# Four tiles of the last stage's input loaded and split inside the attention stage, and ten of its first products issued there

## The chip, the cores and the metric

The kernel runs on one core of a Trainium2 chip. A core has a tensor engine (PE, with its weight loads as PEld), a vector engine (DVE), a scalar engine (ACT), GpSimd (POOL) and SyncE (SP), which here only issues DMAs. The metric is the device time of one execution in microseconds; lower is better.

## The reference

One decoder block with two branches over 2048 positions and 1024 channels, all in float32:

```python
def reference(x, norm_in, w_in, norm_v, w_s, b_s, w_o_gmlp, w_o_sb, w_out, norm_final):
    for layer in range(DEPTH):
        h = rms_norm(x, norm_in[layer])
        proj = jnp.einsum('bsd,de->bse', h, w_in[layer])
        u_a, v_a, z_a, q_b, k_b, v_b, z_b, gate_a, gate_b = jnp.split(proj, SPLIT_POINTS, axis=-1)
        ...
        y_a = chunked_spatial_gating(u_a, v_a, w_s[layer], b_s[layer]) * jax.nn.silu(z_a)
        ...
        y_b = stick_breaking_attention(heads(q_b), heads(k_b), heads(v_b)).reshape(bsz, seq, B_WIDTH)
        y_b = y_b * jax.nn.silu(z_b)
        p_a = jnp.einsum('bse,ed->bsd', y_a, w_o_gmlp[layer])
        p_b = jnp.einsum('bse,ed->bsd', y_b, w_o_sb[layer])
        merged = jax.nn.sigmoid(gate_a) * p_a + jax.nn.sigmoid(gate_b) * p_b
        x = x + jnp.einsum('bsd,de->bse', merged, w_out[layer])
    return rms_norm(x, norm_final)
```

The attention weight of query t for key s is sigmoid(z_ts) times the product of (1 - sigmoid(z_tj)) over the keys j between them.

## The kernel before

Three stages follow each other, each a block of its own; all engines meet at the end of a block. The first makes the norm, the input projection and branch A's mixing. The second, `attention`, makes the stick-breaking attention and, in between, branch A's output projection. The third, `merge_and_project_out`, makes p_b, merges, and projects out.

Every matrix product in float32 precision is three matmuls: each operand is split into a high half (rounded, made by ACT with a copy) and a low half (the rest, made by a subtraction on DVE or POOL), and high·high, high·low and low·high are added in PSUM. A "product" below is such a set of three, with 512 columns.

**Attention.** The work is 320 pieces (8 heads, four blocks of 512 queries taken from the last to the first, key blocks, four rows of 128 queries). All engines follow one list of events in slots. Slot n has event Z for piece n (the logits on PE, L1636 to L1638; two sigmoids on ACT; a scan on DVE, L1566 and L1576; the multiplication by the scanned product on POOL, L1488, after a mask on a diagonal piece), then B for piece n-6 (PE turns the weights, L1661; ACT copies the high half, L1542; DVE makes the low half, L1596), then P for n-8 (the product with v, L1672 to L1674). A turn of a group of four pieces waits until POOL has weighted all four. Behind the 320th piece there are eight more slots, in which only B and P are left. Event Y (L1604, DVE) gates the result of a query block, and SP stores it in `yb_T`.

Operands come through a ring of eight buffers (`RAWS`), as items: q, k, v, branch A's tokens and the weights `w_o_gmlp` ("w") and `w_o_sb` ("o"). SP loads an item when the one eight before it has been split. At the item's own slot (event K) ACT makes the high half (L1510) and POOL the low half (L1476); POOL follows the order of the events too. Items stand in the list `wanted` with the slot of each. The weights of p_b ("o") and two items of q are the last ones.

At the end of attention's program SP waits until all items are split, loads 128x2048 of `yb_T` (the first four tiles of y for the last stage, heads 0 to 3, the last 512 positions) into one wide buffer (L1459), and each of the last four events B is followed by one split of these: ACT's `split_first_chunk` (L1535) and DVE's `rest_of_first_chunk` (L1591).

**Last stage.** For each of four chunks c of 512 positions, from the last, PE adds eight tiles j of y into eight banks k: rows j = 0 to 5 over all k, then per bank j = 6, 7 (L2249 to L2251). DVE gates the banks (`gated_b`, L2153), POOL adds p_a (`add_a`, L1982), ACT issues the store of m_T (L2071). y tiles beyond the first four are loaded through a ring of four and split by ACT (`round_y`, L2044) and DVE (`rest_y`, L2137). POOL first makes four sets of sums of w_out (`w_sums`, L1971 to L1976); SP stores each set (`store_sums`, L1841) and POOL waits for that store before the next set. On SP stand in this order: y tiles 4 to 6 (L1822), w_out piece 0, the store of attention's last result, w_out piece 1, a wait for that store, y 7, eight gates, four p_a (L1832), sums 0, piece 2, sums 1, piece 3, y 8 to 11, sums 2, sums 3, y 12 to 14, the second four p_a, y 15. ACT makes y 4 to 10, then issues the eight stores of chunk 0, then makes y 11; DVE makes the low halves of y 4 to 10, then gates chunk 0. Numbers of y tiles count on over the chunks: y 8 to 15 are chunk 1's.

## Time and profile before

| | |
|---|---|
| median of 3 runs | 2566.29 us (2563.48 to 2568.18) |
| profiled execution | 2569.67 us, span 2568.0 us |
| mean granted clock of PE | 0.990 |
| busy: PE, PEld | 2492.1 us (97%), 2067.6 us (81%) |
| busy: DVE, ACT, POOL | 1596.0 us (62%), 1301.6 us (51%), 1258.3 us (49%) |
| attention ends, last stage starts | 2204.3 us from the span's start |

The span is from the first to the last instruction; the execution has 1.7 us around it. Matmuls are pipelined, so a matmul's own duration (0.39 us) is longer than the distance from one start to the next (0.23 us); distances between starts are what adds up.

### The profile page before, as it was taken

To read this page: it belongs to the slowest core of one execution; us is meant where nothing else is said; L and a number is where in the kernel's file an instruction comes from. 1 tells how busy PE (TensorE), PEld (TensorE's weight loads), DVE (VectorE), ACT (ScalarE), POOL (GpSimd) and SP (SyncE) were. 2 spreads that over 40 slices of the span, in tenths; PEclk is the share of its full clock that TensorE was granted. 3 is DMA by queue.
4 is the path that set the end of the run, shared out by engine and by line. 5 is a ranking of instruction groups with operands and counts; after the bars stand their busy time and mean duration, and the time that the engine had idled before them with its cause. 6 is when DMAs were issued, how large, how long until landed. Compare 5 with 4: busy or idle time off the path is not lost. (4 is left out here: it accounts for less than half of the span.)

```text
span 2568.0 us, 34996 instructions
## 1 busy us (share of the span) xinstructions
PE 2492.1 (97%) x11925; PEld 2067.6 (81%) x11925; DVE 1596.0 (62%) x2091; ACT 1301.6 (51%) x2372; POOL 1258.3 (49%) x1127
## 2 busy tenths in 40 slices
PE   7999999999989999999999999999999999989898
PEld 5788888888878888888888778888888887768687
DVE  7545555554575555555555588878788888332676
ACT  6664333334355444443444387767777778211343
POOL 2543332322335544444343378667866777432564
PEclk9999999999999999999999999999999999999899
DMA  3333333333334345554444434334433433668543
GB/s 123 98 98 119 119 102 115 110 106 122 103 90 127 115 132 151 147 146 144 132 140 127 160 107 141 89 92 138 136 97 106 129 113 101 213 232 276 205 149 113
DMA packets 280633, 338.02 MB, mean 132 GB/s; under 512 B 16408, under 2 KB 181280, under 8 KB 280480
## 3 DMA queue, kind: packets, MB, share of 16 engines
q1 hardware_dynamic: 276880, 329.58, 41.5%
q10 hardware_dynamic: 3600, 6.56, 0.7%
q8 instruction: 77, 1.26, 0.2%
q14 instruction: 76, 0.62, 0.1%
HBM read 222.83 MB, written 113.25 MB: 131 GB/s over the span
## 5 line engine op out<-in xcount | busy, mean ns | idle before, releaser
L1028 PE MATMUL in_bank<-carried_hi,in_w_hi 128*128 128x512 f32 x1988 | 783.4, 394 | 13.1 <-DVE carried_last L822 8.3
L1031 PE MATMUL in_bank<-carried_hi,in_w_lo 128*128 128x512 f32 x1988 | 775.4, 390 | 0.0
L1030 PE MATMUL in_bank<-carried_lo,in_w_hi 128*128 128x512 f32 x1988 | 775.2, 390 | 0.0
L1028 PEld LDWEIGHTS in_bank<-carried_hi,in_w_hi 128*128 128x128 f32 x1988 | 374.1, 188 | 91.9 <-DVE carried_last L822 9.7
L1031 PEld LDWEIGHTS in_bank<-carried_hi,in_w_lo 128*128 128x128 f32 x1988 | 373.9, 188 | 78.9
L1030 PEld LDWEIGHTS in_bank<-carried_lo,in_w_hi 128*128 128x128 f32 x1988 | 374.3, 188 | 74.9
L548 ACT ACTIVATE in_w_hi<-in_sums 128x512 fp32r<-128x512 f32 x284 | 178.6, 630 | 470.1 <-PE in_bank L1031 316.4
L1576 DVE TENSOR_TENSOR_SCAN att_rest<-att_z_ps,att_rest 128x512 f32<-128x512 f32 (+3 forms) x288 | 317.2, 1102 | 47.5 <-ACT att_z_ps L1522 28.6
L417 POOL TENSOR_TENSOR in_sums<-carried_stage 128x512 f32<-128x512 f32 x71 | 97.1, 1367 | 438.7 <-DMA carried_stage<-in_w_in 419.4
L753 DVE TENSOR_TENSOR in_w_lo<-in_sums,in_w_hi 128x512 fp32r<-128x512 f32 x284 | 269.0, 948 | 54.7 <-ACT in_w_hi L548 48.6
L822 DVE TENSOR_TENSOR carried_last<-in_bank,in_o 128x512 f32<-128x512 f32 x71 | 49.1, 691 | 304.6 <-PE in_bank L1031 55.0
L753 DVE TENSOR_TENSOR in_w_lo<-carried_stage,in_w_hi 128x512 fp32r<-128x512 f32 x213 | 214.4, 1007 | 23.5 <-ACT in_w_hi L548 21.5
L548 ACT ACTIVATE in_w_hi<-carried_stage 128x512 fp32r<-128x512 f32 x213 | 133.7, 628 | 144.8 <-PE in_bank L1031 73.3
L1488 POOL TENSOR_TENSOR carried_wide<-carried_wide,att_rest 128x512 f32<-128x512 f32 (+3 forms) x160 | 151.2, 947 | 92.2 <-DVE att_rest L1576 87.5
L1476 POOL TENSOR_TENSOR carried_lo<-carried_wide,carried_hi 128x512 fp32r<-128x512 f32 x152 | 195.4, 1293 | 0.0
L1596 DVE TENSOR_TENSOR att_wT_lo<-att_t_ps,att_wT_hi 128x512 fp32r<-128x512 f32 (+1 forms) x320 | 187.9, 588 | 4.7 <-ACT att_wT_hi L1542 4.4
L1542 ACT ACTIVATE att_wT_hi<-att_t_ps 128x512 fp32r<-128x512 f32 (+1 forms) x320 | 170.4, 533 | 5.1 <-PE att_t_ps L1661 4.8
L1522 ACT ACTIVATE att_z_ps<-att_z_ps 128x512 f32<-128x512 f32 (+2 forms) x320 | 171.3, 535 | 0.0
L1521 ACT ACTIVATE carried_wide<-att_z_ps 128x512 f32<-128x512 f32 (+3 forms) x160 | 85.3, 533 | 83.1 <-PE att_z_ps L1638 82.7
L1672 PE MATMUL att_y_ps<-att_wT_hi,carried_hi 128*128 128x512 f32 (+1 forms) x320 | 120.9, 378 | 3.8 <-DVE carried_wide L1604 2.0
L1636 PE MATMUL att_z_ps<-carried_hi 128*128 128x512 f32 (+2 forms) x320 | 118.1, 369 | 5.0 <-PEq L46 3.7
L1684 PE MATMUL att_f_ps<-carried_hi 128*128 128x512 f32 x256 | 122.1, 477 | 0.0
(215 smaller groups left out, 4787.4 us busy)
## 6 DMA issues: line engine op xcount, KB each, us to landing
carried_stage<-in_w_in SPq DMA_DIRECT2D x144, 512.0 KB, 4.8
carried_wide<-ya_T SPq DMA_DIRECT2D x64, 256.0 KB, 3.4
uz_T<-in_o SPq DMA_DIRECT2D x32, 256.0 KB, 4.6
carried_wide<-va_T SPq DMA_DIRECT2D x16, 512.0 KB, 5.7
carried_wide<-uz_T SPq DMA_DIRECT2D x16, 512.0 KB, 6.3
ya_T<-in_x_sb SPq DMA_DIRECT2D x16, 512.0 KB, 5.0
carried_wide<-k_T SPq DMA_DIRECT2D x32, 256.0 KB, 3.3
carried_wide<-q_T SPq DMA_DIRECT2D x32, 256.0 KB, 3.5
```

The costliest lines, as they stand in the source:

```text
L548: act.activation(w_hi[:, i], left[i], ACT.Copy).then_inc(w_hi_done[i], 1)
L753: dve.tensor_tensor(w_lo[:, i], left[i], w_hi[:, i].bitcast(F32), ALU.subtract)\
L1028: pe.matmul(bank[:, :], hi, a_hi[:, i, k], start=opens and k == 0, stop=False, skip_group_check=True)
L1030: pe.matmul(bank[:, :], hi, a_lo[:, i, k], start=False, stop=False, skip_group_check=True)
L1031: mm = pe.matmul(bank[:, :], lo, a_hi[:, i, k], start=False, stop=k == HALF_K - 1, skip_group_check=True)
L1476: pool.tensor_tensor(lo, src, hi.bitcast(F32), ALU.subtract).then_inc(split_done, 1)
L1488: pool.tensor_tensor(a, a, rest[r][:, left + 1:left + width + 1], ALU.mult).then_inc(weighted, 1)
L1522: act.activation(src, src, ACT.Sigmoid, scale=-SCALE).then_inc(rest_done, 1)
L1542: act.activation(wT_hi[m % W_BUFS][:, c0:], bank_of(step)[:, c0:], ACT.Copy).then_inc(hi_copied, 1)
L1576: dve.tensor_tensor_scan(out=row[:, left:left + width][:, ::-1], data0=z_ps[n % Z_BANKS][:, 0:width][:, ::-1], data1=row[:, S:S + 1].to_br ...
L1596: dve.tensor_tensor(wT_lo[b][:, c0:], bank_of(step)[:, c0:], wT_hi[b][:, c0:].bitcast(F32), ALU.subtract).then_inc(lo_copied, 1)
L1684: pe.matmul(f_ps[:, :], wo_hi[:, j, cols], ya_hi[:, j], start=j == 0, stop=False)
```

## The change

The first four tiles of y become items of attention's ring ("y", at slots 306, 309, 317 and 312 for tiles 0, 1, 2, 3), each loaded alone; ACT makes the high half at that slot and POOL the low half. The wide load and the splits behind the last four events B go away. Ten of the first 64 products of the last stage (tile j, bank k) become events M on PE in slots 311, 313, 316 and 320 to 326, each at the end of its slot, into banks 0 to 3. For this the eight PSUM banks are shared by all stages; the last stage's bank 0 is attention's `f_ps`, banks 1 to 3 its `z_ps`. The last stage leaves these ten out, and its counters of split y tiles start at tile 4.

```diff
+FIRST_Y = [306, 309, 317, 312]
+EARLY_M = {(0, 0): 311, (1, 0): 313, (3, 0): 316, (2, 0): 320, (0, 1): 321, (0, 2): 322, (0, 3): 323, (1, 1): 324,
+           (1, 2): 325, (1, 3): 326}
...
+        for j in range(QT):
+            wanted.append((FIRST_Y[j], ("y", j, 0)))
...
+            order += [("M", jk) for jk, at_slot in EARLY_M.items() if at_slot == slot]
...
+    if which == "y":
+        return s["yb_T"][m * P:(m + 1) * P, S - CW:S]
...
+    if which == "y":
+        return carried.first_chunk(m)
...
-        z_ps = [sc.ps(f"z_ps{n}", [P, CW]) for n in range(Z_BANKS)]
-        t_ps = [sc.ps(f"t_ps{n}", [P, CW]) for n in range(T_BANKS)]
-        y_ps, f_ps = sc.ps("y_ps", [P, CW]), sc.ps("f_ps", [P, CW])
+        z_ps, t_ps = carried.banks[:Z_BANKS], carried.banks[Z_BANKS:Z_BANKS + T_BANKS]
+        y_ps, f_ps = carried.banks[-2:]
...
+                if item[0] == "y":
+                    for n in range(ZBS):
+                        sp.wait_ge(y_stored[n], 16 * len(range(n, item[1] * NSUP + 1, ZBS)))
...
-            last_sup = range((HEADS - 1) * NSUP + 1)
-            for n in range(ZBS):
-                sp.wait_ge(y_stored[n], 16 * len(last_sup[n::ZBS]))
-            sp.wait_ge(split_done, len(splits))
-            sp.wait_ge(split_first, len(by_vector))
-            sp.wait_ge(turned, max(w.step_of["V", item] for item in w.items if item[0] == "v") + 1)
-            first_y = carried.buffer[1].rearrange("p (j t) -> p j t", j=QT)
-            sp.dma_start(first_y, s["yb_T"].rearrange("(j p) t -> p j t", p=P)[:, 0:QT, S - CW:S])\
-                .then_inc(carried.y_loaded, 16)
...
+                elif which == "y":
+                    place = FIRST_PLACES[m]
+                    act.wait_ge(z_full, w.last_logits(("qk"[place // QT], HEADS - 1, place % QT)) + 1)
...
-                if m >= len(w.turns) - QT:
-                    split_first_chunk(m - len(w.turns) + QT)
...
-                if m >= len(w.turns) - QT:
-                    rest_of_first_chunk(m - len(w.turns) + QT)
...
+            def first_chunk(j, k):
+
+                if k == 0:
+                    pe.wait_ge(f_done, BLOCKS)
+                else:
+                    pe.wait_ge(scanned, max(n for n in range(len(w.pieces)) if n % Z_BANKS == k - 1) + 1)
+                wait_split(pe, ("y", j, 0), ("o", k, j // (KT // 2)))
+                bank, cols = [f_ps, *z_ps][k], slice(k * P, (k + 1) * P)
+                y_hi, y_lo = carried.first_chunk(j)
+                opens = (j, k) == next(jk for jk in EARLY_M if jk[1] == k)
+                pe.matmul(bank[:, :], wo_hi[:, j, cols], y_hi, start=opens, stop=False, skip_group_check=True)
+                pe.matmul(bank[:, :], wo_hi[:, j, cols], y_lo, start=False, stop=False, skip_group_check=True)
+                pe.matmul(bank[:, :], wo_lo[:, j, cols], y_hi, start=False, stop=False, skip_group_check=True)
...
-        banks = [sc.ps(f"bank{i}", [P, CW]) for i in range(BANKS)]
+
+        banks = [carried.banks[-1], *carried.banks[:-1]]
...
-                sp.wait_ge(y_lo_done, n - RING + 1)
+                if n >= RING + QT:
+                    sp.wait_ge(y_lo_done, n - RING + 1 - QT)
...
+                        if c == 0 and (j, k) in EARLY_M:
+                            continue
```

GpSimd's own order, at slots 304 to 308. Before, L1488 is the weighting of a piece, L1484 the mask, L1476 the low half of an item (here of "o"):

```order
L1488 TENSOR_TENSOR carried_stage<-carried_stage,att_rest 128x512 x2
L1476 TENSOR_TENSOR carried_lo<-carried_wide,carried_hi 128x4x128
L1488 TENSOR_TENSOR carried_wide<-carried_wide,att_rest 128x512
L1488 TENSOR_TENSOR att_slot<-att_slot,att_rest 128x512
L1476 TENSOR_TENSOR carried_lo<-carried_wide,carried_hi 128x4x128
```

With the change the same operations are L1494 and L1482:

```order
L1494 TENSOR_TENSOR carried_stage<-carried_stage,att_rest 128x512 x2
L1482 TENSOR_TENSOR carried_lo<-carried_wide,carried_hi 128x4x128
L1494 TENSOR_TENSOR carried_wide<-carried_wide,att_rest 128x512
L1482 TENSOR_TENSOR carried_lo<-carried_wide,carried_hi 128x512
L1494 TENSOR_TENSOR att_slot<-att_slot,att_rest 128x512
L1482 TENSOR_TENSOR carried_lo<-carried_wide,carried_hi 128x4x128
```

The low half of y's tile 0 (the 128x512 row) now stands between the weighting of pieces 306 and 307; those of tiles 1 and 3 stand likewise behind pieces 309 and 312, that of tile 2 behind piece 317.

The tensor engine's order, from the turn of piece 316 (slot 322) on. Before, L1661 turns (one row of this list per source tile), L1672 to L1674 are one product with v:

```order
L1661 MATMUL att_t_ps<-carried_ident,carried_wide 128x128
L1661 MATMUL att_t_ps<-carried_ident,att_slot 128x128 x2
L1661 MATMUL att_t_ps<-carried_ident,carried_last 128x128
L1672 MATMUL att_y_ps<-att_wT_hi,carried_hi 128x512
L1673 MATMUL att_y_ps<-att_wT_lo,carried_hi 128x512
L1674 MATMUL att_y_ps<-att_wT_hi,carried_lo 128x512
L1661 MATMUL att_t_ps<-carried_ident,att_slot 128x128 x2
L1661 MATMUL att_t_ps<-carried_ident,carried_last 128x128
```

With the change the turns are L1655, the products with v L1666 to L1668, and the new events M L1692 to L1694:

```order
L1655 MATMUL carried_bank<-carried_ident,carried_wide 128x128
L1655 MATMUL carried_bank<-carried_ident,att_slot 128x128 x2
L1655 MATMUL carried_bank<-carried_ident,carried_last 128x128
L1666 MATMUL carried_bank<-att_wT_hi,carried_hi 128x512
L1667 MATMUL carried_bank<-att_wT_lo,carried_hi 128x512
L1668 MATMUL carried_bank<-att_wT_hi,carried_lo 128x512
L1692 MATMUL carried_bank<-carried_hi 128x512
L1693 MATMUL carried_bank<-carried_lo,carried_hi 128x512
L1694 MATMUL carried_bank<-carried_hi,carried_lo 128x512
L1655 MATMUL carried_bank<-carried_ident,att_slot 128x128 x2
L1655 MATMUL carried_bank<-carried_ident,carried_last 128x128
```

A product of the last stage now stands between the product of piece 314 and the turn of piece 317. The same holds after the products of pieces 315, 316, 317 and 318; one more M stands right ahead of the turn of piece 316 (slot 321), and one right ahead of the turn of piece 315 (slot 320).

## Rows read from the trace of the kernel before

**Rows 1.** The page's first part: busy us, share, instructions.

```profile
PE 2492.1 (97%) x11925; PEld 2067.6 (81%) x11925; DVE 1596.0 (62%) x2091; ACT 1301.6 (51%) x2372; POOL 1258.3 (49%) x1127
```

**Rows 2.** Busy time by stretch: stretch, its length, each engine's busy us (instructions).

```profile
core 0: us, PE busy (x) PEld busy (x) DVE busy (x) ACT busy (x) POOL busy (x), PEclk, DMA share, GB/s
2158.30:2192.90 34.60, 31.20 (x172) 24.84 (x171) 31.10 (x44) 30.23 (x67) 34.09 (x37) 1.00 0.21 61
...
2204.30:2248.30 44.00, 43.81 (x193) 36.01 (x193) 6.50 (x9) 4.43 (x7) 15.83 (x13) 1.00 0.79 277
2248.30:2265.00 16.70, 16.60 (x72) 13.40 (x72) 4.03 (x7) 0.00 (x0) 10.07 (x8) 1.00 0.61 205
2265.00:2274.20 9.20, 0.01 (x1) 0.01 (x1) 0.76 (x2) 1.42 (x3) 4.92 (x4) 0.65 0.66 245
2274.20:2280.00 5.80, 5.80 (x18) 4.66 (x19) 2.43 (x4) 1.41 (x3) 0.00 (x0) 0.68 0.62 180
```

**Rows 3.** The tensor engine's waits in the last stage: total us, times, longest.

```profile
PE b_bank L2260 <- DVE carried_wide L2182: 11.2, 1, 11.2
PE b_bank L2249 <- DVE carried_lo L2137: 9.3, 1, 9.3
```

**Rows 4.** The chain that ended last, 2204 to 2275 us: start, us, what.

```profile
2204.32 0.32 SPq L1822
...
2206.11 7.31 DMA yb_T<-carried_wide
...
2221.33 8.71 DMA w_sums<-b_sums
...
2246.42 4.27 DMA w_sums<-b_sums
...
2255.94 5.04 POOL carried_wide L1982 x4
...
2263.00 6.43 DMA carried_wide<-pa_T
...
2273.44 1.90 DVE carried_lo L2137 x3
```

**Rows 5.** DVE in order of time: start, us, count, idle before it.

```profile
2203.34 0.69 DVE L1604 TENSOR_TENSOR carried_wide<-att_y_ps,carried_wide 128x512 f32<-128x512 f32 x1
...
2247.47 4.86 DVE L2153 TENSOR_TENSOR carried_wide<-b_bank,carried_wide 128x512 f32<-128x512 f32 x8
```

**Rows 6.** GpSimd's groups of instructions, 2158.3 to 2197.2 us.

```profile
L1476 POOL TENSOR_TENSOR carried_lo<-carried_wide,carried_hi 128x512 fp32r<-128x512 f32 x12 | 15.5, 1296 | 0.0
```

**Rows 7.** GpSimd in order of time, its last pieces of attention.

```profile
2187.91 1.28 POOL L1476 TENSOR_TENSOR carried_lo<-carried_wide,carried_hi 128x512 fp32r<-128x512 f32 x1
2189.14 2.15 POOL L1488 TENSOR_TENSOR carried_stage<-carried_stage,att_rest 128x512 f32<-128x512 f32 x2
...
2194.00 0.87 POOL L1488 TENSOR_TENSOR att_slot<-att_slot,att_rest 128x384 f32<-128x384 f32 x1 [0.77 <-DVE att_rest L1576]
...
2196.06 1.09 POOL L1488 TENSOR_TENSOR carried_last<-carried_last,att_rest 128x512 f32<-128x512 f32 x1 [0.94 <-DVE att_rest L1576]
```

**Rows 8.** The tensor engine in order of time, attention's last turns and products.

```profile
2197.35 0.27 PE L1661 MATMUL att_t_ps<-carried_ident,carried_wide 128*128 128x128 f32 x1
...
2199.62 0.27 PE L1661 MATMUL att_t_ps<-carried_ident,carried_last 128*128 128x128 f32 x1
2200.65 0.47 PE L1672 MATMUL att_y_ps<-att_wT_hi,carried_hi 128*128 128x512 f32 x1 [0.76 <-DVE carried_wide L1604]
...
2202.30 0.28 PE L1674 MATMUL att_y_ps<-att_wT_hi,carried_lo 128*128 128x256 f32 x1
2202.75 0.33 PE L1672 MATMUL att_y_ps<-att_wT_hi,carried_hi 128*128 128x128 f32 x1 [0.17 <-DVE att_wT_lo L1596]
...
2204.35 0.47 PE L2249 MATMUL b_bank<-carried_hi 128*128 128x512 f32 x1 [1.05 <-PEq L1354]
```

**Rows 9.** DVE's group of the first four tiles' low halves, 2197 to 2204.3 us.

```profile
L1591 DVE TENSOR_TENSOR carried_lo<-carried_wide,carried_hi 128x512 fp32r<-128x512 f32 x4 | 2.7, 679 | 0.0
```

More of the change, by code:

```diff
@@ L162, in norm_and_project @@
         v_mean, v_rms = (sc.sb(n, [P, NT]) for n in ("v_mean", "v_rms"))
-        banks = [sc.ps(f"bank{i}", [P, CW]) for i in range(BANKS)]
+        banks = carried.banks
         stage = carried.as_weights(0)
@@ L1258, in in_slots @@
                 wanted.append((free, ("o", c, part)))
-        wanted.sort(key=lambda w: (w[0], w[1][1], -w[1][2], "kqvawo".index(w[1][0])))
+        for j in range(QT):
+            wanted.append((FIRST_Y[j], ("y", j, 0)))
+        wanted.sort(key=lambda w: (w[0], w[1][1], -w[1][2], "kqvawoy".index(w[1][0])))
         self.items = [item for _, item in wanted]
@@ L1529, in copy_v @@
                 act.activation(halves_of(carried, item)[0], bank_of(step)[:, :], ACT.Copy).then_inc(hi_copied, 1)
-            def split_first_chunk(i):
-                src, hi, _ = carried.first_chunk(i)
-                act.wait_ge(carried.y_loaded, 16)
-                act.wait_ge(z_full, len(w.pieces))
-                act.activation(hi, src, ACT.Copy).then_inc(carried.y_hi_done, 1)
             def copy_weights(m):
@@ L1586, in rest_of_v @@
                 dve.tensor_tensor(lo, bank_of(step)[:, :], hi.bitcast(F32), ALU.subtract).then_inc(lo_copied, 1)
-            def rest_of_first_chunk(i):
-                src, hi, lo = carried.first_chunk(i)
-                dve.wait_ge(carried.y_hi_done, i + 1)
-                dve.tensor_tensor(lo, src, hi.bitcast(F32), ALU.subtract).then_inc(carried.y_lo_done, 1)
             def rest_of_weights(m):
@@ L1690, in _ @@
                     logits(i)
+                elif e == "M":
+                    first_chunk(*i)
                 elif e == "V":
@@ L1751, in merge_and_project_out @@
         minus_half = sc.sb("minus_half", [P, 1])
-        banks = [sc.ps(f"bank{i}", [P, CW]) for i in range(BANKS)]
+        banks = [carried.banks[-1], *carried.banks[:-1]]
         bank_a, bank_b, bank_c = ([banks[3 * b + j] for b in range(2)] for j in range(3))
@@ L1785, in merge_and_project_out @@
         y_loaded, gate_loaded, pa_loaded = sc.sems("y_loaded", RING), sc.sems("gate_loaded", KT), sc.sems("pa_loaded", RING)
-        y_hi_done, y_lo_done = carried.y_hi_done, carried.y_lo_done
+        y_hi_done, y_lo_done = sc.sem("y_hi_done"), sc.sem("y_lo_done")
         row_done, full, gated, added = (sc.sem(n) for n in ("row_done", "full", "gated", "added"))
@@ L1859, in load_m @@
                 if n == 0:
-                    sp.wait_ge(y_lo_done, TILES_Y)
+                    sp.wait_ge(y_lo_done, TILES_Y - QT)
                 elif n == 1:
@@ L2135, in rest_y @@
             def rest_y(n):
-                dve.wait_ge(y_hi_done, n + 1)
+                dve.wait_ge(y_hi_done, n + 1 - QT)
                 dve.tensor_tensor(y_half(1, n), y_raw[n % RING], y_half(0, n).bitcast(F32), ALU.subtract)\
@@ L2248, in outer @@
                 n = KT * c + j
-                pe.matmul(banks[k][:, :], wo(0, j, k), y_half(0, n), start=j == 0, stop=False, skip_group_check=True)
+                opens = j == 0 and (c > 0 or k not in (of for _, of in EARLY_M))
+                pe.matmul(banks[k][:, :], wo(0, j, k), y_half(0, n), start=opens, stop=False, skip_group_check=True)
                 pe.matmul(banks[k][:, :], wo(0, j, k), y_half(1, n), start=False, stop=False, skip_group_check=True)
@@ L2267, in _ @@
                 for j in range(BY_HEAD):
-                    pe.wait_ge(y_lo_done, KT * c + j + 1)
+                    wait_past(pe, y_lo_done, max(0, KT * c + j + 1 - QT))
                     for k in range(KT):
@@ L2276, in _ @@
                         if k == 0:
-                            pe.wait_ge(y_lo_done, KT * c + j + 1)
+                            pe.wait_ge(y_lo_done, KT * c + j + 1 - QT)
                         mm = outer(c, j, k)
@@ L2325, in __init__ @@
         self.ident = sc.sb("ident", [P, P])
+        self.banks = [sc.ps(f"bank{i}", [P, CW]) for i in range(BANKS)]
         self.not_older = sc.sb("not_older", [P, P])
@@ L2335, in __init__ @@
         self.y_stored = sc.sems("y_stored", ZBS)
-        self.y_loaded, self.y_done, self.y_hi_done, self.y_lo_done = (
-            sc.sem(n) for n in ("y_loaded", "y_done", "y_hi_done", "y_lo_done"))
+        self.y_done = sc.sem("y_done")
     def first_chunk(self, i):
@@ L2342, in first_chunk @@
         cols = slice(place % 4 * CW, (place % 4 + 1) * CW)
-        return [self.buffer[1][:, i * CW:(i + 1) * CW], self.hi[:, place // 4, cols], self.lo[:, place // 4, cols]]
+        return [half[:, place // 4, cols] for half in (self.hi, self.lo)]
     def as_tiles(self, n):
```

## Prediction, made before the changed kernel ran

> **What bounds the kernel now.** I first read the page: the tensor engine is busy for 97% of the span [rows 1]. That is an average, and the change works at one seam, so I then read busy time by stretch around the end of attention, the waits of the tensor engine behind it, the chain of work that ended last, and each engine in order of time.
>
> In the last 35 us of attention's pieces the engine without a pause is not the tensor engine but GpSimd: 34.09 us busy of 34.60, against 31.20 for PE [rows 2]. All of this stretch's weighting and splitting queues there, and PE's turns wait for it.
>
> In the last stage PE runs without a gap for 44 us, for another 16.7 us with a hardly visible one, and then stands still for 9.2 us [rows 2, 3]. What it waits for is tile 11 of y, the fourth of chunk 1. The chain shows why that tile is late, and none of it is PE: SP's first issue at 2204.32, the store of attention's last result (7.31 us), SP's further issues, the store of the first sums (8.71 us), GpSimd's sums and their stores in turns until 2255.94, four additions of p_a, the load of the next four p_a (6.43 us), their additions, ACT's stores, and the split of tile 11 at 2273.44 [rows 4]. The chain begins with the block itself; nothing in it waits for a product of chunk 0. From there on PE is the bound except for one wait of 11.2 us, for the first output sums [rows 3], which hangs on the chunks before it.
>
> So there are two clocks. The end of attention moves everything behind it. What PE saves between 2204 and 2265 is not worth anything, as it only comes earlier to the wait for tile 11.
>
> **What is saved in the last stage.** In that stage PE makes 193 matmuls in 44.00 us, one per 0.228 us [rows 2]. Ten products are thirty matmuls, 6.84 us. Chunk 0 would be done 6.8 us earlier after the stage's start, at about 2241.4 on the old scale. But chunk 1's first product needs bank 0 gated, and DVE starts that at 2247.47, right behind the low half of tile 10 [rows 5], whose load SP issues in its fixed order. PE so waits there for some 7 us, makes three rows, and then waits for tile 11 as before. If the clock falls in the first wait, as it does in the 9.2 us one (granted clock 0.65, and 0.68 in the 5.8 us behind it, which is the 1.2 GHz level for a part of them [rows 2]), the rows behind it take some 2 us longer, and there are 9 us of waiting to hide that. Term: 0. If that cover were not there, the term would be -6.8.
>
> The order of loads changes nothing here: y 4 to 7 had their buffers free before too, and the counters for y 8 on ask for the same tiles.
>
> **GpSimd's four low halves.** One costs 1.296 us by its own record [rows 6]; from one start to the next instruction's it is 1.23 (2187.91 to 2189.14 [rows 7]). I take 1.24. In the stretch in which tiles 0, 1 and 3 are inserted (behind pieces 306, 309, 312) GpSimd is never idle for long, so the weighting of piece 315 is 3 x 1.24 = 3.7 us later. Tile 2's half stands behind piece 317. There GpSimd waits twice for scans, 0.77 and 0.94 us [rows 7], and those scans hang on piece 319's logits, which PE makes behind the turn of piece 312, thus behind the weighting of piece 315: from the end of that one (2189.14 + 2.15 = 2191.29) to the end of the last (2196.06 + 1.09 = 2197.15) it is 5.86 us, of which GpSimd works 5.86 - 1.71 = 4.15. With 1.24 more it works 5.4, which fits. So the fourth costs nothing, and the last weighting moves by 3.7. Bounds: 5.0 if all four count, 0 if the queue had slack. Queued behind GpSimd are PE's turns, and behind these ACT and DVE.
>
> What this takes off DVE is four low halves of 0.679 us [rows 9], and four copies off ACT. They lie in the last 6 us, where DVE and ACT wait for PE's turns in between; the gating that product 316 waits for comes at most 0.2 us earlier by it. Bounds 0 to 1; I take 0.
>
> The Trainium skill's GPSIMD Engine Reference (Engine selection) advises VectorE for elementwise work on a tile, since GpSimd takes about twice as long for two inputs. The trace agrees: 1296 ns against 679 ns for the same subtraction. By that rule alone the four halves would cost 4 x 0.6 = 2.5 us more of engine time, whoever waits for it.
>
> **PE behind the last weighting.** Before, from the turn of piece 316 (2197.35) to the last product (2202.75) there are 5.40 us. Two waits are in it, by starts: 2199.62 + 0.11 to 2200.65 is 0.92, 2202.30 + 0.12 to 2202.75 is 0.33 [rows 8]. PE works 4.15 us. The change puts five products (slots 322 to 326) between these, 5 x 0.684 = 3.4 us, and one (slot 321) right ahead of the turn of piece 316, where PE arrives just as the weighting ends: 0.7 us. The first wait shrinks to some 0.2 us, because it is what is left of the time from product 315 to the gating of its block's result (0.92 and 0.23 of piece 318's turn, 1.15), and now a product and the turn lie in that (0.68 + 0.23); the second goes. New length 0.7 + 4.15 + 3.4 + 0.2 = 8.45, against 5.40: 3.05 us later. The products of slots 311, 313, 316 and 320 are hidden: PE has 3.4 us of gaps in the 34.6 before [rows 2] and now waits more for GpSimd. Bounds: 4.1 if no wait shrinks, about 2.3 if the turn of 316 doesn't find PE occupied.
>
> **The sum.** Attention ends 3.7 + 3.05 = 6.75 us later. The last gated result starts at 2203.34 [rows 5] and the stage's first matmul at 2204.35 [rows 8], 1.0 us apart with the meeting of the engines between them; this distance stays. The last stage keeps its length. The profiled execution of 2569.67 would become 2576.4; it stands 3.4 us above the median 2566.29, to which the same difference is added: 2573.0 us, slower by 0.26%.
>
> **The rivals.**
> - *GpSimd has slack after all* (its pieces are due later than I think, so that its late halves don't reach PE): only the 3.05 us of the tail stay, 2569.3. For it: PE is 31.2 us busy of 34.6, so it doesn't wait much. Against it: a queue with 0.5 us of idle time in 34.6 has nothing to take 5 us in. It decides if the weighting of piece 319 ends less than 1.5 us later. Chance 0.12.
> - *The saving shows in the last stage too, and pays the seam*: 6.75 - 6.84, 2566.2. That would need the wait for tile 11 to follow PE, not SP. For it: 97% of PE in the span. Against it: the chain [rows 4]. Chance 0.08.
> - *Faster*: the seam's work lies in PE's waits (they sum to 3.4 us in the stretch and 1.3 in the tail) and the thirty matmuls leave the path behind it. If chunk 0's end is what releases chunk 1's gating, and so tile 11, each product saved counts 0.68 us; it turns faster by over 0.2% when attention's end moves by less than 1.7 us. With an end that doesn't move: 2559.5. Against it: DVE's gating began at 2247.47 right behind a low half, before PE had asked for it. Chance 0.06. The Trainium skill's Perfetto Trace Analysis (Optimization Strategy) says that interleaving regimes with different bounds may gain; this rival is that rule at work, and the trace speaks against it, as the regime that receives the work has a full queue on GpSimd.
> - *The clock*: the new wait of 7 us and the old one stand 16 us apart. If PE stays at the lower clock in the rows between, or longer behind tile 11, each 4 us at it cost 2 us. Behind tile 11 that is not hidden: 2575 to 2577. Chance 0.08.
> - *My forecast*, 0.66, with a range of its own of 2570.0 to 2576.0.
>
> **How the numbers follow.** What a measurement of this kernel can tell from no change is about 0.2%, 5.1 us; the three runs spread over 4.7 us. Slower by that is above 2571.4. Of the forecast's 0.66 about 0.50 lies above it, since the tail or the queue may be 1.5 us shorter than I make it; with the clock's 0.08 that is 0.58. Within 0.2%: 0.16 of the forecast, 0.12 and 0.08, 0.36. Faster 0.06. The range reaches down to the rival without a change, less some noise, 2565.5, and up to the clock's 2577.0; about 0.1 stays out on either side.
>
> **What would show it.** Right, if in the changed kernel GpSimd is busy without a gap from 2158 to about 2196 and its last weighting ends near 2201; if DVE's last gating of attention starts near 2210 and the last stage's first matmul near 2211; if PE has a new wait of 6 to 8 us there, released by DVE's gating of chunk 0, and still 7 to 10 us for tile 11, which ends near 2281; and if the stretch from the stage's first matmul to the end is as long as before within 1.5 us. Wrong, if the last stage is shorter by several us: then something in SP's chain followed PE. Wrong in the first term, if GpSimd shows waits among pieces 306 to 317, and in the second, if PE's gaps behind the last weighting stay.

## The result and the profile after

The changed kernel takes 2573.11 us (median of 8 runs, 2571.66 to 2575.56) against 2566.11 us of the kernel before (8 runs, the three on record among them, 2563.11 to 2570.37): 7.0 us slower, a ratio of 1.0028 with a 95% interval of 1.0018 to 1.0037. The profiled execution took 2574.6 us with a span of 2572.9 us.

This profile ran 2.6 us ahead of the one before when it reached the change. 2.5 of it was there when attention's first matmul started (1474.69 against 1477.18 us), and in the fourteen profiles that start lies anywhere from 1474.69 to 1479.78, with the change and without. So I compare distances, not places. GpSimd in order of time, before and then after, with piece 305 (the second of the x2 in the first row) as the common mark, since the first new item comes behind it:

```profile
2171.01 2.17 POOL L1488 TENSOR_TENSOR carried_stage<-carried_stage,att_rest 128x512 f32<-128x512 f32 x2
```

```profile
2168.44 2.15 POOL L1494 TENSOR_TENSOR carried_stage<-carried_stage,att_rest 128x512 f32<-128x512 f32 x2
...
2172.85 1.28 POOL L1482 TENSOR_TENSOR carried_lo<-carried_wide,carried_hi 128x512 fp32r<-128x512 f32 x1
...
2190.29 2.15 POOL L1494 TENSOR_TENSOR carried_stage<-carried_stage,att_rest 128x512 f32<-128x512 f32 x2
...
2194.11 1.28 POOL L1482 TENSOR_TENSOR carried_lo<-carried_wide,carried_hi 128x512 fp32r<-128x512 f32 x1
...
2197.22 1.09 POOL L1494 TENSOR_TENSOR carried_last<-carried_last,att_rest 128x512 f32<-128x512 f32 x1 [0.39 <-DVE att_rest L1577]
```

Before, piece 305's weighting ends at 2173.18 and the last weighting at 2197.15 [rows 7], 23.96 us apart (from unrounded times). After, it is 2170.59 to 2198.31, 27.72: GpSimd's part of attention's end is 3.76 us longer. The low half of tile 0 (2172.85) and its neighbours stand in a queue with no pause; that of tile 2 (2194.11) stands where the waits of 0.77 and 0.94 us were [rows 7], and only one of 0.39 is left.

The tensor engine in order of time behind the last weighting (L1655 turns, L1666 to L1668 products with v, L1692 to L1694 the new ones, L2263 the last stage):

```profile
2199.20 0.27 PE L1655 MATMUL carried_bank<-carried_ident,carried_wide 128*128 128x128 f32 x1
...
2202.85 0.27 PE L1655 MATMUL carried_bank<-carried_ident,carried_last 128*128 128x128 f32 x1
2203.09 0.47 PE L1666 MATMUL carried_bank<-att_wT_hi,carried_hi 128*128 128x512 f32 x1
...
2206.70 0.39 PE L1694 MATMUL carried_bank<-carried_hi,carried_lo 128*128 128x512 f32 x1
2206.93 0.22 PE L1666 MATMUL carried_bank<-att_wT_hi,carried_hi 128*128 128x128 f32 x1
...
2208.43 0.47 PE L2263 MATMUL carried_bank<-carried_hi 128*128 128x512 f32 x1 [1.05 <-PEq L1367]
```

From the turn of piece 316 to the last product it is 2199.20 to 2206.93, 7.73 us, against 5.40 [rows 8]; the turn comes 0.89 us behind the last weighting, against 0.20. The wait of 0.92 us by starts is now 2202.85 + 0.11 to 2203.09, 0.13, and the other is gone. DVE in order of time shows attention's last gating (L1598) and the first of chunk 0 (L2166):

```profile
2207.41 0.69 DVE L1598 TENSOR_TENSOR carried_wide<-carried_bank,carried_wide 128x512 f32<-128x512 f32 x1 [1.95 <-PE carried_bank L1668]
...
2251.89 4.87 DVE L2166 TENSOR_TENSOR carried_wide<-carried_bank,carried_wide 128x512 f32<-128x512 f32 x8
```

From the last weighting to the last gating it is 9.10 us against 6.19: the tail is 2.91 us longer. Together attention ends 6.67 us later, and the first matmul stands 1.02 us behind that gating as before.

Busy time by stretch in the last stage, and the tensor engine's waits there:

```profile
core 0: us, PE busy (x) PEld busy (x) DVE busy (x) ACT busy (x) POOL busy (x), PEclk, DMA share, GB/s
...
2208.30:2252.30 44.00, 37.00 (x162) 30.33 (x162) 5.77 (x8) 4.42 (x7) 15.19 (x13) 0.95 0.80 280
2252.30:2271.50 19.20, 18.78 (x71) 15.32 (x72) 4.46 (x8) 0.00 (x0) 10.53 (x9) 0.84 0.66 227
```

```profile
PE carried_bank L2274 <- DVE carried_wide L2195: 11.0, 1, 11.0
PE carried_bank L2263 <- DVE carried_wide L2166: 9.6, 2, 7.3
PE carried_bank L2263 <- DVE carried_lo L2150: 5.8, 1, 5.8
```

The first 44 us hold 162 matmuls instead of 193 [rows 2], and the last stage has a new wait of 7.3 us for the gating of chunk 0. The other part of the 9.6 us is the wait for the gating of chunk 1: 2.3 us, ending 101.3 us behind the stage's first matmul, against 2.15 us and 101.2 before. The wait for tile 11 is 5.8 us instead of 9.3 [rows 3] and ends 69.4 us behind the stage's first matmul, against 69.8. The stage takes 364.5 us from its first matmul to the end, against 363.6. So the saving of 6.84 us is there in PE's work and nowhere in the time. Against the profile before, the sum is 6.67 + 0.86 - 2.6 = 4.9 us, the difference of the spans.

### The profile page after: what moved, and what is told of

It reads as the page before. It is cut to its first block and busy times, and to the rows that moved or that the text cites. A ratio compares the mean times of both kernels' runs of the same rounds, so it can differ in the third digit from the quotient of the medians.

```text
span 2572.9 us, 35013 instructions
## 1 busy us (share of the span) xinstructions
PE 2497.2 (97%) x11925; PEld 2071.5 (81%) x11925; DVE 1593.6 (62%) x2087; ACT 1302.9 (51%) x2372; POOL 1270.1 (49%) x1131
## 5 line engine op out<-in xcount | busy, mean ns | idle before, releaser
L1028 PE MATMUL carried_bank<-carried_hi,in_w_hi 128*128 128x512 f32 x1988 | 783.8, 394 | 11.1 <-DVE carried_last L822 8.2
L1031 PE MATMUL carried_bank<-carried_hi,in_w_lo 128*128 128x512 f32 x1988 | 775.9, 390 | 0.0
L1030 PE MATMUL carried_bank<-carried_lo,in_w_hi 128*128 128x512 f32 x1988 | 775.5, 390 | 0.0
L1028 PEld LDWEIGHTS carried_bank<-carried_hi,in_w_hi 128*128 128x128 f32 x1988 | 374.4, 188 | 89.5 <-DVE carried_last L822 9.7
L1031 PEld LDWEIGHTS carried_bank<-carried_hi,in_w_lo 128*128 128x128 f32 x1988 | 374.2, 188 | 78.9
L1030 PEld LDWEIGHTS carried_bank<-carried_lo,in_w_hi 128*128 128x128 f32 x1988 | 374.6, 188 | 75.2
L1577 DVE TENSOR_TENSOR_SCAN att_rest<-carried_bank,att_rest 128x512 f32<-128x512 f32 (+3 forms) x288 | 317.5, 1103 | 48.2 <-ACT carried_bank L1531 28.9
L1482 POOL TENSOR_TENSOR carried_lo<-carried_wide,carried_hi 128x512 fp32r<-128x512 f32 x156 | 200.4, 1292 | 0.0
L1494 POOL TENSOR_TENSOR carried_wide<-carried_wide,att_rest 128x512 f32<-128x512 f32 (+3 forms) x160 | 151.1, 946 | 91.7 <-DVE att_rest L1577 87.1
L1592 DVE TENSOR_TENSOR att_wT_lo<-carried_bank,att_wT_hi 128x512 fp32r<-128x512 f32 (+1 forms) x320 | 188.6, 590 | 7.2 <-ACT att_wT_hi L1545 6.8
L1545 ACT ACTIVATE att_wT_hi<-carried_bank 128x512 fp32r<-128x512 f32 (+1 forms) x320 | 170.5, 533 | 9.1 <-PE carried_bank L1655 8.9
L1531 ACT ACTIVATE carried_bank<-carried_bank 128x512 f32<-128x512 f32 (+2 forms) x320 | 171.2, 535 | 0.0
L1666 PE MATMUL carried_bank<-att_wT_hi,carried_hi 128*128 128x512 f32 (+1 forms) x320 | 120.8, 377 | 2.3 <-DVE carried_wide L1598 1.3
```

The source lines that it names most:

```text
L1028: pe.matmul(bank[:, :], hi, a_hi[:, i, k], start=opens and k == 0, stop=False, skip_group_check=True)
L1030: pe.matmul(bank[:, :], hi, a_lo[:, i, k], start=False, stop=False, skip_group_check=True)
L1031: mm = pe.matmul(bank[:, :], lo, a_hi[:, i, k], start=False, stop=k == HALF_K - 1, skip_group_check=True)
L1482: pool.tensor_tensor(lo, src, hi.bitcast(F32), ALU.subtract).then_inc(split_done, 1)
L1494: pool.tensor_tensor(a, a, rest[r][:, left + 1:left + width + 1], ALU.mult).then_inc(weighted, 1)
L1531: act.activation(src, src, ACT.Sigmoid, scale=-SCALE).then_inc(rest_done, 1)
```

## The experiments

Each kernel ran in turns with the kernel before. One profile's last stage varies by some us between executions even where its code is the same: e2 and the change have the same last stage, with 359.9 and 364.5 us. Up to e9 the part behind the wait for the first output sums is always 154.7 to 155.8 us long; what varies is when that wait ends, 204.5 to 209.3 us behind the stage's first matmul. So a difference of less than some 5 us in one profile's last stage says nothing by itself. The ratio judges the whole, and the profile's distances judge attention's end, which repeats within 0.05 us. A "lock" below is a wait that ends when it did, whatever work of PE ahead of it is taken away. In the table these are: from the end of piece 305's weighting to the end of the last weighting; from there to the last gating's start; from the stage's first matmul to the end of the span. The ratio is to the kernel before.

| kernel | us, median | ratio, 95% interval | queue | tail | last stage |
|---|---|---|---|---|---|
| before | | | 23.96 | 6.19 | 363.6 |
| change | 2573.11 | 1.0028 (1.0018 to 1.0037) | 27.72 | 9.10 | 364.5 |
| e1_no_early | 2569.25 | 1.0007 (0.9997 to 1.0016) | 27.75 | 5.72 | 361.7 |
| e2_low_dve | 2573.25 | 1.0029 (1.0017 to 1.0040) | 25.69 | 9.12 | 359.9 |
| e3_four_early | 2570.12 | 1.0017 (1.0007 to 1.0026) | 27.73 | 5.74 | 359.5 |
| e4_left_out | 2565.65 | 0.9993 (0.9983 to 1.0002) | 23.99 | 6.19 | 361.1 |
| e5_act_order | 2568.85 | 1.0004 (0.9994 to 1.0013) | 23.98 | 6.19 | 360.2 |
| e6_act_order_after | 2573.49 | 1.0021 (1.0011 to 1.0030) | 27.73 | 9.13 | 360.6 |
| e8_loads_before | 2567.33 | 1.0000 (0.9990 to 1.0009) | 23.96 | 6.20 | 363.3 |
| e9_loads_after | 2572.56 | 1.0016 (1.0006 to 1.0025) | 27.74 | 9.10 | 363.4 |
| e10_w_later_before | 2559.49 | 0.9973 (0.9963 to 0.9984) | 23.96 | 6.19 | 356.2 |
| e11_w_later_after | 2568.41 | 1.0003 (0.9994 to 1.0013) | 27.73 | 9.10 | 357.4 |
| e12_w_later_four | 2567.18 | 1.0004 (0.9994 to 1.0013) | 30.93 | 5.73 | 357.1 |
| e13_w_later_four_pool | 2565.52 | 0.9991 (0.9982 to 1.0001) | 27.74 | 5.75 | 356.5 |

The kernel before that ran beside them had medians of 2566.11 us (change), 2566.75 (e1 to e4), 2567.36 (e5 to e9), 2566.03 (e10 to e12) and 2567.16 (e13).

**The two terms apart.** No early products at all:

```diff
-EARLY_M = {(0, 0): 311, (1, 0): 313, (3, 0): 316, (2, 0): 320, (0, 1): 321, (0, 2): 322, (0, 3): 323, (1, 1): 324,
-           (1, 2): 325, (1, 3): 326}
+EARLY_M = {}
```

> The change without its ten early products (the table of them is empty; the last stage makes all 64 again); the four y tiles stay items of attention's ring with low halves by GpSimd. Two-term theory (GpSimd's queue 3.7 us, products in the tail 3.0 us): only GpSimd's term is left, attention's last weighting still ends 3.7 us later against piece 305, the last gated result 3.2 to 3.7 us later (DVE and ACT lack the old splits in the tail), the last stage is as long as before; time 3.5 us above before, 3.5 below the change. Rival A (the products alone cost, GpSimd has slack): as before, 2566. Rival B (the products pay in the last stage and GpSimd costs all of it): not below the change, 2573 or more.

The queue stays 3.79 us longer, the tail is 0.47 us shorter than before. GpSimd's first and last rows of the distance, and DVE's last gating (L1597):

```profile
2168.93 2.15 POOL L1493 TENSOR_TENSOR carried_stage<-carried_stage,att_rest 128x512 f32<-128x512 f32 x2
...
2197.73 1.09 POOL L1493 TENSOR_TENSOR carried_last<-carried_last,att_rest 128x512 f32<-128x512 f32 x1 [0.37 <-DVE att_rest L1576]
```

```profile
2204.54 0.69 DVE L1597 TENSOR_TENSOR carried_wide<-carried_bank,carried_wide 128x512 f32<-128x512 f32 x1 [0.64 <-PE carried_bank L1667]
```

Attention ends 3.3 us later. The time, 2.5 us above before by the medians with an interval of the ratio of -0.8 to 4.1, agrees with that and is clear of the change. Both rivals fall: the queue shows that GpSimd has no slack (the time alone would still allow no difference), and the time lies below the change, so the products do cost. The 0.47 us is what went with the four old splits on ACT and DVE; I had taken 0.

With only the four early products that I had called hidden:

```diff
+EARLY_M = {(0, 0): 311, (1, 0): 313, (3, 0): 316, (2, 0): 320}
```

> The change with only four early products, those of slots 311, 313, 316 and 320; the six of slots 321 to 326 go back to the last stage. Two-term theory: these four lie in waits, so it is as the change without any: last weighting 3.7 us later, tail no longer than before (5.2 to 5.4 us from the turn of piece 316 to the last product, change 8.3), time 3.5 us above before and equal to the kernel without early products within 0.5 us. Rival (each of the ten costs alike, 0.3 us apiece, as PE is 97% busy): 1.2 us above the kernel without.

The queue is 27.73 and the tail 5.74, within 0.02 us of the kernel without any; the time is 0.9 us above that one's, less than the two intervals can tell apart. These four cost nothing in attention, and the six of slots 321 to 326 cost all of the 3.4 us by which the tails of change and e3 differ.

Low halves of y by DVE at the same slots (a counter of its own, `y_low`, on which PE and SP wait for these items):

```diff
+                if e == "K" and i[0] == "y":
+                    hi, lo = halves_of(carried, i)
+                    dve.wait_ge(split_hi, hi_of[i] + 1)
+                    dve.tensor_tensor(lo, raw_of(i)[0], hi.bitcast(F32), ALU.subtract).then_inc(y_low, 1)
```

> The change with the four low halves of y made by DVE at the same slots instead of GpSimd; the ten early products stay. Two-term theory: GpSimd's queue is relieved of 4 x 1.24 us, DVE gets 4 x 0.59 us with 3.5 us of idle time in that stretch; the last weighting is 0 to 1 us later than before (change: 3.7), the tail is 3.0 us longer as in the change; the last gated result 3.0 to 4.0 us later than before, time 3.5 us above before. Rival A (GpSimd has slack): no better than the change, 2573. Rival C (DVE is as full, the scans come late): 6 us above before.

This missed. The queue shrinks from 27.72 to 25.69, but is still 1.73 us longer than before, more than the 0 to 1 expected; the tail is 9.12. The time is 6.5 us above before (interval 4.4 to 10.3) instead of 3.5, and no better than the change. The rows of GpSimd and DVE show where the 1.73 us come from:

```profile
2171.46 2.59 POOL L1500 TENSOR_TENSOR carried_stage<-carried_stage,att_rest 128x512 f32<-128x512 f32 x2
...
2177.36 1.75 POOL L1488 TENSOR_TENSOR carried_lo<-carried_wide,carried_hi 128x512 fp32r<-128x512 f32 x1
...
2184.85 1.41 POOL L1500 TENSOR_TENSOR carried_wide<-carried_wide,att_rest 128x512 f32<-128x512 f32 x1
...
2190.80 2.15 POOL L1500 TENSOR_TENSOR carried_stage<-carried_stage,att_rest 128x512 f32<-128x512 f32 x2
```

```profile
2172.03 1.07 DVE L1618 TENSOR_TENSOR carried_lo<-carried_wide,carried_hi 128x512 fp32r<-128x512 f32 x1
...
2177.27 0.69 DVE L1618 TENSOR_TENSOR carried_lo<-carried_wide,carried_hi 128x512 fp32r<-128x512 f32 x1
...
2184.56 0.74 DVE L1618 TENSOR_TENSOR carried_lo<-carried_wide,carried_hi 128x512 fp32r<-128x512 f32 x1
```

Each of these three subtractions overlaps an instruction of GpSimd, and that instruction is longer than its like in the change: 2.59, 1.75 and 1.41 us instead of 2.15, 1.28 and 1.09, 1.2 us together. By as much the weighting of pieces 314 and 315 starts late: 19.34 us behind that of 304 and 305, against 18.13 before. Behind it GpSimd loses 0.9 us more, with a new wait of 0.72 us for a scan of DVE. So all of it is 2.1 us; piece 305's end, the mark of the table, hides 0.4 us, since its own row is one of the longer ones.

**Is PE's saving worth anything in the last stage?** The kernel before with the ten products left out altogether, so that its p_b lacks them (the first product left in each bank opens it):

```diff
+LEFT_OUT = [(0, 0), (1, 0), (2, 0), (3, 0), (0, 1), (0, 2), (0, 3), (1, 1), (1, 2), (1, 3)]
...
+                        if c == 0 and (j, k) in LEFT_OUT:
+                            continue
```

> The kernel before, whose last stage leaves out the ten products (tiles 0 to 3 into banks 0 to 3) altogether, so that p_b lacks them for the first chunk; attention is untouched. Theory (the wait for tile 11 hangs on SP, GpSimd and the stores): no gain, time within 1.5 us of before; a new wait of 6 to 8 us on DVE's gating of chunk 0, and the wait for tile 11 ends at the same distance from the stage's start, 69 to 70 us. Rival (the last stage follows PE): 6.8 us below before, 2559.

It is 1.1 us below before, with an interval of -4.4 to 0.5 us; a gain of 6.8 us is excluded. The tensor engine's waits in the last stage:

```profile
PE b_bank L2262 <- DVE carried_wide L2183: 10.1, 1, 10.1
PE b_bank L2250 <- DVE carried_wide L2154: 8.0, 2, 6.6
PE b_bank L2250 <- DVE carried_lo L2138: 6.9, 1, 6.9
```

The work left out has become a wait of 6.6 us for the gating of chunk 0. The wait for tile 11 ends 68.6 us behind the stage's first matmul (69.8 before), and that for the gating of chunk 1 at 100.1 (101.2 before). So even work that vanishes, with no cost elsewhere, had gained only 1.1 us by then.

**Which lock is it?** On ACT in the last stage, tile 11 goes ahead of the stores:

```diff
             for n in range(4, 11):
                 round_y(n)
-            for k in range(KT):
+            round_y(11)
+            for k in range(RING):
                 store_m(0, k)
-            for n in range(11, 16):
+            for n in range(12, 15):
                 round_y(n)
+            for k in range(RING, KT):
+                store_m(0, k)
+            round_y(15)
```

> The kernel before with one reordering on ACT in the last stage: the split of tile 11 stands ahead of the eight stores of chunk 0, tiles 12 to 14 between the fourth and the fifth, tile 15 behind them. Theory (tile 11 is late because ACT's stores wait for the additions of p_a): the wait for tile 11 of 9.3 us goes, and the last stage gets 6 to 10 us shorter, unless the wait before the first output sums (11.2 us, about 205 us behind the stage's start) grows by what is gained; time 2557 to 2560. Rival (tile 11 is late for its load or for DMA bandwidth): no change, 2566. Rival 2 (the later wait grows by the same): 2566 with that wait at 18 to 20 us.

This missed: there is no gain (1.5 us above, interval -1.5 to 3.3), though the mechanism worked: tile 11 is ready 48.5 us behind the stage's start instead of 69.8, and PE never waits for it. Its waits now:

```profile
PE b_bank L2253 <- DVE carried_wide L2157: 11.5, 1, 11.5
PE b_bank L2264 <- DVE carried_wide L2186: 8.4, 1, 8.4
```

The 9.3 us moved into the wait for the gating of chunk 1 (2.15 us before), which now ends 98.8 us behind the start. It was neither of the two waits that I had thought of. The same reordering on the changed kernel:

> The changed kernel with the same reordering on ACT. Theory: its last stage has the same gain, but the wait for the gating of chunk 0 (7.3 us) stays, for that hangs on the loads of tiles 8 to 10; so it stands 6.7 us above the kernel before with the reordering, as without it. Rival (with tile 11 out of the way the ten early products pay): equal to the kernel before with the reordering within 1.5 us.

It stands 4.6 us above e5 by the medians (4.4 by the ratios), attention ends 6.7 us later, and it has both the 7.2 us wait for chunk 0's gating and one of 9.5 us for chunk 1's.

Then SP's loads, on both kernels: tiles 8 to 10 right behind tile 7, tile 11 behind w_out's piece 2, tiles 12 to 14 behind piece 3.

```diff
             load_y(7)
+            for n in range(8, 11):
+                load_y(n)
...
             load_piece(2)
+            load_y(11)
             store_sums(1)
             load_piece(3)
-            for n in range(8, 12):
-                load_y(n)
+            for n in range(12, 15):
+                load_y(n)
             store_sums(2)
             store_sums(3)
-            for n in range(12, 15):
-                load_y(n)
```

> The kernel before with the reordering on ACT and SP's loads of tiles 8 to 10 right behind that of tile 7, tile 11 behind w_out's piece 2, tiles 12 to 14 behind piece 3. Theory: DVE can gate chunk 0 as soon as PE closes its banks; for the kernel before this is worth nothing over the reordering alone (PE met no wait there), 0 to 1 us either way. Rival (the earlier loads delay the sums of w_out on the full DMA queues): some us slower than the reordering alone.

> The changed kernel with both, the reordering on ACT and the earlier loads of y. Theory: only here nothing is left to wait for in the first two chunks, so the thirty matmuls moved out of the last stage count, 6.8 us, against 6.7 us of later attention end: equal to the kernel before with both within 1.5 us, its waits after the stage's start at about 44 and 69 us gone. Rival (another chain holds the last stage, the sums of w_out or the stores of m_T): 6.7 us above the kernel before with both, with the wait before the first output sums grown by 6 to 7 us.

e8 equals before. In e9 the wait at 44 us is gone, as expected, and the kernel is still 5.2 us above e8 by the medians, 4.1 by the ratios. With the width of the two intervals that leaves room for a part of the saving, so the waits have to decide:

```profile
PE carried_bank L2268 <- DVE carried_wide L2171: 16.6, 1, 16.6
PE carried_bank L2279 <- DVE carried_wide L2200: 11.0, 1, 11.0
PE carried_bank L2268 <- DVE carried_lo L2155: 1.7, 1, 1.7
```

e8 waits 11.3 us for the gating of chunk 1. There are 16.6 - 11.3 + 1.7 = 7.0 us of new waits: the 6.84 us saved, all of it. The rival was right that another chain holds the stage, though not in which: the wait before the first output sums did not grow (11.0 us, e8 11.7). The lock that takes everything ahead of it is the gating of chunk 1. In before, the change and e1 to e9 PE's wait for it ends 98.6 to 101.8 us behind the stage's first matmul, whatever was changed ahead of it; the waits at 44 and 70 us were only its forerunners.

**Moving that lock.** On ACT the splits of w_out's blocks for chunks 1 and 2 go behind the six y tiles, on DVE behind the gating too:

```diff
-                for i in (P1, P6) if c == 1 else (P2,):
-                    rest_w(i)
                 for j in range(BY_HEAD):
                     rest_y(KT * (c + 1) + j)
                 for k in range(KT):
                     gated_b(c, k)
+                for i in (P1, P6) if c == 1 else (P2,):
+                    rest_w(i)
```

> The kernel before with tile 11 ahead of the stores on ACT, the earlier loads of y on SP, and on ACT and DVE the splits of w_out's blocks for chunks 1 and 2 behind the six y tiles (on DVE behind the gating too). Theory (the gating of chunk 1, about 100 us behind the stage's start, is the lock on which all savings ahead of it are lost; it is late because on ACT and DVE the two blocks of w_out stand ahead of y 16 to 21 and the gating): the wait of 11.3 us at 99 us shrinks to 2 to 4 us, the last stage is 7 to 9 us shorter, 2558 to 2560. Rival (a later lock, the wait before the first output sums at 205 us, takes it back): 2566, with that wait near 18 us.

It takes 2559.49 us, 0.9973 (0.9963 to 0.9984): the fastest of all, 6.5 us below before. Its waits:

```profile
PE b_bank L2265 <- DVE carried_wide L2187: 9.8, 1, 9.8
PE b_bank L2254 <- DVE carried_wide L2158: 6.3, 1, 6.3
```

11.3 us became 6.3, less than I expected to be taken off, and the wait before the first output sums did not grow. In this profile ACT's split ahead of the gating waits 19 us for loads of y that SP issues behind the two blocks of w_out. So the lock has moved by 5 us (the wait ends 93.6 us behind the start instead of 98.6) and is still one. The other 2 us of the 7.1 by which the stage is shorter than e8's go with the wait before the first output sums (9.8 us instead of 11.7), and are within what that varies by. The changed kernel with the same:

> The changed kernel with the same three. Theory: with the locks loosened a part of the 6.8 us saved on PE can count; but what is left as a wait in the kernel before with the three (2 to 4 us) shows that the loads are nearly as late, so only that remainder is missed: 3 to 6.7 us above the kernel before with the three. Rival (nothing else holds): equal to it within 1.5 us. Rival 2 (a lock remains and takes all): 6.7 us above it.

It is 8.9 us above e10, 7.7 us by the ratios. Attention's end is 6.7 us of it; the last stage shows no saving (357.4 us, against 356.2), with a wait of 10.1 us for the gating of chunk 1, which ends at 92.4 us. I had expected 3 to 6.7; the second rival holds, the lock still takes all.

The changed kernel with the same three, the four hidden products alone and y's low halves by DVE:

> The changed kernel with the same three, only the four early products that lie in waits, and y's low halves by DVE. Theory: attention ends 1.3 us later than before (last weighting +1.7, tail -0.4), four products (2.7 us) fewer in the last stage: between 1.4 us below and 1.3 us above the kernel before with the three, about 2558 to 2561, and faster than both given kernels. Rival (as above, a lock takes all): 1.3 us above the kernel before with the three, and no faster than before.

This missed: 2567.18 us, 8.0 above e10 by the ratios, where 1.4 below to 1.3 above was expected. The tail is as expected (5.73), but the queue is 30.93 us, 7.0 longer than before, where e2 with the same subtractions had 1.7. DVE's first subtraction of y, and GpSimd in order of time beside it:

```profile
2167.93 4.43 DVE L1617 TENSOR_TENSOR carried_lo<-carried_wide,carried_hi 128x512 fp32r<-128x512 f32 x1
2172.29 0.68 DVE L1597 TENSOR_TENSOR att_wT_lo<-carried_bank,att_wT_hi 128x512 fp32r<-128x512 f32 x1
```

```profile
2167.36 2.18 POOL L1499 TENSOR_TENSOR carried_stage<-carried_stage,att_rest 128x512 f32<-128x512 f32 x2
2169.47 1.30 POOL L1487 TENSOR_TENSOR carried_lo<-carried_wide,carried_hi 128x512 fp32r<-128x512 f32 x1
2170.69 1.13 POOL L1499 TENSOR_TENSOR carried_wide<-carried_wide,att_rest 128x512 f32<-128x512 f32 x1
2174.23 1.09 POOL L1499 TENSOR_TENSOR att_slot<-att_slot,att_rest 128x512 f32<-128x512 f32 x1 [2.42 <-DVE att_rest L1582]
```

The subtraction took 4.43 us; the other seven of e2 and e12 took 0.67 to 1.07. It reads two tiles in SBUF and ends 0.54 us after GpSimd's run of four instructions (2170.69 + 1.13 = 2171.82); the next DVE instruction reads one of its tiles from PSUM and takes 0.68. Behind it DVE's scans came late and GpSimd stood still for 2.42 us, and further on for 0.64, 0.91, 0.75 and 1.12 us. Why this one subtraction and none of the seven others took so long is not shown. To tell this from an effect of the early products or the reorderings, the same kernel with low halves by GpSimd:

> The changed kernel with the three reorderings and the four early products that lie in waits, but y's low halves by GpSimd, as in the change. It tells apart why the same kernel with low halves by DVE lost: there the last weighting came 7 us late with one subtraction on DVE of 4.4 us. Theory (that subtraction reads two tiles in SBUF while GpSimd does too, and its length is a matter of chance): here the last weighting comes 3.7 to 3.8 us late, the tail is 0.4 us shorter, attention ends 3.3 us later than before; the last stage has the length of the one with DVE, 357 us, since a lock about 94 us behind its start still takes the four products; time 3 to 4 us above the kernel before with the three reorderings, about 2563. Rival (the reorderings with the early products make attention's end late): last weighting 6 to 7 us late here too.

The queue is 27.74, the tail 5.75, the last stage 356.5: each as the theory had it, and the rival falls. So the 7.0 us came with DVE's subtractions. The time is 2565.52 us, 0.9991, 4.6 us above e10 by the ratios, a bit more than the 3 to 4 expected, within the intervals.

## Why the prediction was right

**The sum.** 6.75 us were predicted for the end of attention and 6.67 measured; the time was 2573.0 against 2573.11. The agreement of the distances is worth something, since they repeat within 0.05 us. That of the times to 0.1 us is luck: the difference of 7.0 us has an interval of 4.6 to 9.5, and the profiled execution was predicted at 2576.4 and took 2574.6. With the 2.6 us by which that profile ran ahead added, the places fit too: last weighting 2200.9 (about 2201 predicted), last gating 2210.0 (2210), first matmul 2211.0 (2211).

**GpSimd's four low halves.** 3.7 us were predicted, 3.76 measured in the change and 3.79 alone (e1). Three count and the fourth lies in the waits for the scans. From the weighting of pieces 304 and 305 to that of 314 and 315 it is 2168.44 to 2190.29, 21.85 us, against 2171.01 to 2189.14, 18.13 [rows 7]: 3.72, three times 1.24. Behind that only 0.04 is added, and of the waits 0.39 us is left. The rule of the Trainium skill that elementwise work belongs on VectorE (GPSIMD Engine Reference, Engine selection) is right on an instruction's length (0.68 against 1.30 us). As a remedy it gave little here: with the subtractions on DVE the queue is 2.0 us shorter than the change's in e2, but 3.2 longer in e12 than in e13, and no run of it is faster than its partner on GpSimd. The instructions of the two engines held each other up there.

**PE behind the last weighting.** 3.05 us were predicted, 2.91 measured. The mechanism is as predicted (the first wait shrinks to 0.13 us, the second goes), but the closeness is partly luck: the six products cost 3.4 us (e3 against the change), 0.3 more than the term, and the removal of the old splits gives back 0.47, which I had put at 0 with a bound of 1.

**The last stage keeps its length.** This was right, and shown by e4 with no other part of the change in it. But the reason as the prediction put it was too short. It said that tile 11 is the lock and that from there on PE is the bound except for the wait of 11.2 us. That failed in e5: tile 11 came 21 us earlier and nothing was gained, since the gating of chunk 1 is a second lock behind it. With tile 11 out of the way, the same reasoning gave a wrong forecast for e9. The waits of before had the sign of it in a row that I passed over as small (the gating of chunk 1, 101 us behind the stage's start):

```profile
PE b_bank L2249 <- DVE carried_wide L2153: 2.1, 1, 2.1
```

A wait of 2 us says only that PE came 2 us too early; it doesn't say that 2 us is all that can be lost there.

**The new wait.** For the gating of chunk 0, 6 to 8 us were predicted and 7.3 measured. Tile 11's wait was predicted at 7 to 10 us and measured 5.8, so this sign missed: behind the new wait PE had the 1.2 GHz level for its first 12 starts or so (0.43 us apart instead of 0.23), which costs some 2.5 us, and they went off the next wait. The granted clock of the stretch shows the lower level, 0.84 against 1.00 before [rows 2]. The prediction had some 2 us for this; the rest of the miss is that the new wait is 0.4 us longer than the 6.84 saved, and that tile 11 came 0.5 us earlier. The clock's rival, a cost behind tile 11, didn't come: that wait ends 0.5 us earlier than before, and the next one in the same place (101.3 us).

**The rivals.** GpSimd's slack: refuted by e1. The saving that pays in the last stage, and the faster case: refuted by e4 in the time, and by the waits of e9 and e11, in which two other arrangements of the stage took it back.

## What to carry to other kernels

Before moving work off an engine, find the last lock behind it, not the first. Remove the work altogether in an experiment: if that gains nothing, moving it can't either. An engine with 49% over the span can be the one without a pause where the work is to go; read the stretch, and count each item that is queued behind it. A wait that is filled with work holds only as much as it is long: four of the ten products here were free, the six at the very end cost 0.56 us each, 3.36 together.

## What the runs showed of the hardware

A subtraction on DVE with both sources in SBUF took 4.43 us in e12 (0.67 to 1.07 in seven other cases of e2 and e12) while GpSimd ran four instructions on SBUF without a pause, and ended 0.54 us after the last of them. It goes the other way too: in e2 GpSimd's instructions that overlapped such a subtraction took 0.3 to 0.5 us longer than their like in the change. Before, the same subtraction took 0.68 us with GpSimd idle [rows 9]. The Trainium skill's SBUF — State Buffer (SBUF: two separate sides) describes this as a lock that one engine holds for a whole instruction and not a sharing of bandwidth. These rows agree with one engine holding up the other; that the wait lasted through several GpSimd instructions in a row, and not one, is how I read the one case of 4.43 us, and no second case shows it.
